# Differential attention: rotation among the projections, heads written out, maxima of the next head ahead of the present head's mixing

## What is computed

```python
ql, kl, vl = project(hl)          # latent tokens, 8 heads, q and k of 2 x 64, v of 128
qc, kc, vc = project(hc)          # context tokens
ql, kl = apply_rope(ql, cos, sin), apply_rope(kl, cos, sin)      # only the latent ones
lam = exp(sum(lp[0]*lp[1])) - exp(sum(lp[2]*lp[3])) + lam_init
keys, vals = concatenate([kc, kl]), concatenate([vc, vl])        # 512 tokens
s = einsum('bqhmd,bkhmd->bhmqk', q, keys) * 64 ** -0.5           # m = 0, 1
p = softmax(s)
a = p[:, :, 0] - lam * p[:, :, 1]
o = einsum('bhqk,bkhe->bqhe', a, vals)
y = rmsnorm(o, subln) * (1 - lam_init)                           # then @ w_out
```

## Time and profile before

| | us |
|---|---|
| median of three runs | 2550.07 |
| the profiled execution, its time | 2550.66 |
| its span, from the first to the last instruction | 2549.0 |
| TensorE busy in the span | 2421.8 |
| VectorE busy | 828.5 |
| ScalarE busy | 528.4 |
| GpSimd busy | 195.4 |

### The profile page before, as it was taken

One profiled execution on the slowest core, in us unless ns is written; L12 is line 12 of the kernel. 1 busy time (PEld: TensorE's weight loads), 2 busy tenths in 40 slices (PEclk: granted clock), 3 DMA queues, 4 the chain that ended last, 5 costly groups with the idle time before them and its releaser, 6 DMA issues.

```text
span 2549.0 us, 31145 instructions
## 1 busy us (share of the span) xinstructions
PE 2421.8 (95%) x12399; PEld 1977.2 (78%) x12399; DVE 828.5 (33%) x1600; ACT 528.4 (21%) x1305; POOL 195.4 (8%) x268
## 2 busy tenths in 40 slices
PE   5999999999998999899999999999999999678998
PEld 3788888864556988778888888888888867367887
DVE  4233310164545777253333013433301200731001
ACT  2111110122233444331111103111110211431001
POOL 1100000001022232000001000000000000100000
PEclk7999999999999999999999999999999999988999
DMA  8554462412210000134446523522452231023462
GB/s 271 199 174 156 163 169 73 136 53 81 67 50 17 1 1 1 50 117 148 165 151 192 168 68 106 186 95 82 128 136 68 89 116 66 0 66 119 158 173 62
DMA packets 277449, 275.56 MB, mean 108 GB/s; under 512 B 6505, under 2 KB 258019, under 8 KB 277219
## 3 DMA queue, kind: packets, MB, share of 16 engines
q1 hardware_dynamic: 256611, 198.60, 25.6%
q0 software_dynamic: 20736, 75.51, 8.4%
HBM read 273.04 MB, written 1.05 MB: 108 GB/s over the span
## 4 chain that ended last, share of the span: by engine, by line
PE 91%; DVE 4%; ACT 3%; issue 2%; DMA 1%; SPq 0%; POOL 0%; POOLq 0%; DVEq 0%; ACTq 0%
PE bank L714 32%; PE bank L859 18%; PE bank L609 12%; PE bank L879 6%; PE bank L905 3%; PE bank L1026 2%; PE bank L681 2%; PE bank L587 2%; PE bank L1185 2%; PE bank L1033 2%; PE bank L964 1%; PE bank L1040 1%; PE bank L989 1%; ACT hs L1571 1%; DVE room L2003 1%
## 5 line engine op out<-in xcount | busy, mean ns | idle before, releaser
L859 PE MATMUL bank<-big,ring 128*128 128x256 f32 x2112 | 458.8, 379 | 0.0
L859 PEld LDWEIGHTS bank<-big,ring 128*128 128x128 f32 x2112 | 400.4, 190 | 53.9
L714 PE MATMUL bank<-hs,ring 128*128 128x256 f32 x1584 | 378.3, 384 | 1.3 <-ACT hs L1316 1.3
L714 PEld LDWEIGHTS bank<-hs,ring 128*128 128x128 f32 x1584 | 300.1, 192 | 52.2 <-issue 11.3
L714 PE MATMUL bank<-room,big 128*128 128x256 f32 x1056 | 252.5, 382 | 0.0
L609 PE MATMUL bank<-hs,ring 128*128 128x512 f32 (+2 forms) x592 | 231.6, 548 | 0.0
L714 PEld LDWEIGHTS bank<-room,big 128*128 128x128 f32 x1056 | 201.8, 192 | 28.1 <-DVE room L1780 0.5
L2188 DVE TENSOR_TENSOR room<-room 128x256 f32<-128x256 f32 x70 | 29.8, 425 | 521.0 <-ACT room L1607 521.0
L609 PEld LDWEIGHTS bank<-hs,ring 128*128 128x128 f32 (+1 forms) x592 | 109.8, 188 | 107.6 <-issue 104.1
L472 POOL DMA_DIRECT2D mring<-in_w_mod x144 | 76.2, 529 | 1084.1 <-PE bank L587 1009.8
L879 PE MATMUL bank<-hs,ring 128*128 128x256 f32 x704 | 153.9, 382 | 1.6 <-ACT hs L1316 1.6
(11 more groups left out here) (277 smaller groups left out, 2826.2 us busy)
## 6 DMA issues: line engine op xcount, KB each, us to landing
ring<-in_ffn_w_in SPq DMA_DIRECT2D x88, 1024.0 KB, 5.0
mring<-in_w_mod POOLq DMA_DIRECT2D x144, 512.0 KB, 5.4
ring<-in_ffn_w_out SPq DMA_DIRECT2D x44, 1408.0 KB, 7.0
ring<-in_gdn_w_in SPq DMA_DIRECT2D x16, 1024.0 KB, 5.5
ring<-in_diff_w_in SPq DMA_DIRECT2D x12, 1024.0 KB, 5.1
ring<-in_gdn_w_out SPq DMA_DIRECT2D x4, 1024.0 KB, 4.9
ring<-in_diff_w_out SPq DMA_DIRECT2D x4, 1024.0 KB, 4.9
cst<-in_consts SPq DMA_DIRECT2D x1, 1344.0 KB, 9.5
```

The source lines that it names most:

```text
L714: last = mm(bank[:, (g0 + b) % 4, 0:LAT], w[:, k, jj * P:(jj + 1) * P], rhs[:, k, :], start=start and k == 0, stop=(k == KC // 2 - 1), ski ...
L859: last = mm(bank[:, g % 4, 0:LAT], w[:, k, :], big[:, k, cols], start=(k == 0), stop=(k == FC - 1))
```

## The change

The rotation leaves the heads. `turn_back(i)` and `rotary(i)` now handle one key or query block each (i = 0 to 7 keys, 8 to 15 queries) and write the result back to `big` in place. TensorE issues the first two behind `first_four`, one behind each of the twelve following groups of keys and queries, and the last two behind the first two groups of values. VectorE runs its 16 rotations ahead of everything for lambda. `scores` reads q and k from `big` directly, and the values product reads `v_rows`, so GpSimd's copies are gone. The heads are written out one by one on all engines. VectorE runs `maxima(h+1)` and then `mix(h)`; ScalarE runs `exps(h+1)` ahead of the copies of head h. Scores of head 0 no longer wait for lambda. `oat`, `rat` and the bank of the values product alternate between two buffers. New waits guard the transposes (`a_copied` of the head before), the mix (`a_turned` of the head before) and the copies (`attn_done` of the head before).

```diff
@@ room
-        qrot = carve(LAT)
-        rtmp = carve(2, LAT)
-        rtmp2 = carve(2, LAT)
-        vhead = [carve(NC, P), carve(NC, P)]
-        kall = [carve(TOK), carve(TOK)]
+        rtmp = [carve(LAT), carve(LAT)]
+        rtmp2 = [carve(LAT), carve(LAT)]
...
-        oat = carve(LAT)
-        rat = carve(LAT)
+        oat = [carve(LAT), carve(LAT)]
+        rat = [carve(LAT), carve(LAT)]
@@ GpSimd
             pool.wait_ge(S["head_closed"], HEADS + 2)
-            for par in range(2):
-                k_fix(par, par)
-                v_fix_rows(par, par)
...
+            for h in range(HEADS):
+                of("attn_root", h, 1, 1)
+                nc.gpsimd.tensor_tensor(big[:, h + 3 * KC, 0:LAT], oat[h % 2], rat[h % 2], ALU.mult).then_inc(S["head_closed"], 1)
@@ TensorE
+                    def turn_back(i):
+
+                        pe.wait_ge(S["acc_freed"], g0 + i + 1 + 4)
+                        if i > 1:
+                            pe.wait_ge(S["rotated"], i - 1)
+                        x = big[:, KC + i, CTX:TOK] if i < KC else big[:, i - KC, 0:LAT]
+                        mm(bank[:, 4 + i % 2, 0:LAT], k_("rot"), x, start=True, stop=True).then_inc(S["turned_back"], 1)
+
+                    for i in range(2):
+                        turn_back(i)
...
+                                turn_back(part * 8 + 2 * r + jj - 2)
...
+                            if r == 0 and t < 2:
+                                turn_back(2 * KC - 2 + t)
...
-                    def scores(n, par, first=False):
-                        of("k_fixed", n, 1, 1)
-                        of("rotated", n, 2, 2)
+                    def scores(n):
...
-                    def one_head(h, par, more):
-                        if more:
-                            turn_back(h + 1)
-                            scores(h + 1, 1 - par)
+                    def attend(h):
                         for t in range(2):
                             of("mixed_done", h, 2, t + 1)
+                            if h:
+                                of("a_copied", h - 1, 2, t + 1)
...
+                    pe.wait_ge(S["rotated"], 2 * KC)
+                    scores(0)
                     pe.wait_ge(S["head_closed"], HEADS + 2)
-                    turn_back(0)
-                    scores(0, 0, first=True)
-                    heads_of(lambda n: pe.Fori(0, n), one_head)
+                    pe.wait_ge(S["acc_freed"], g0 + 32 + 4)
+                    for h in range(HEADS):
+                        if h + 1 < HEADS:
+                            scores(h + 1)
+                        attend(h)
@@ ScalarE
+                    exps(0, range(4))
+                    act.wait_ge(S["head_closed"], HEADS + 2)
+                    for h in range(HEADS):
+                        if h + 1 < HEADS:
+                            exps(h + 1, range(4))
+                        copy_a(h)
+                        leave(h)
+                        root(h)
@@ VectorE
+                    def rotary(i):
+
+                        x = big[:, KC + i, CTX:TOK] if i < KC else big[:, i - KC, 0:LAT]
+                        dve.wait_ge(S["acc_freed"], g0 + i + 1 + 4)
+                        steps.did(v_.tensor_tensor(rtmp[i % 2], x, k_("cos"), ALU.mult))
+                        dve.wait_ge(S["turned_back"], i + 1)
+                        steps.link(v_.tensor_tensor(rtmp2[i % 2], bank[:, 4 + i % 2, 0:LAT], k_("sin"), ALU.mult))
+                        v_.tensor_tensor(x, rtmp[i % 2], rtmp2[i % 2], ALU.add).then_inc(S["rotated"], 1)
+
+                    for i in range(2 * KC):
+                        rotary(i)
+
...
+                            if h:
+                                of("a_turned", h - 1, 2, t + 1)
...
-                        if more:
-                            maxima(h + 1, 1 - par)
...
+                    maxima(0)
+                    for h in range(HEADS):
+                        if h + 1 < HEADS:
+                            maxima(h + 1)
+                        mix(h)
```

More of the change, by code:

```diff
@@ L1206, in scores @@
                                 rows = slice(m * HALF, (m + 1) * HALF)
-                                if not first:
+                                if n:
                                     of("probs_done", n - 1, 4, 2 * t + m + 1)
-                                mm(bank[:, 4 + 2 * t + m, :], qrot[rows, t * P:(t + 1) * P], kall[par][rows, :], start=True, stop=True).then_inc(S["scores_done"], 1)
-                    def one_head(h, par, more):
-                        if more:
-                            turn_back(h + 1)
-                            scores(h + 1, 1 - par)
+                                mm(bank[:, 4 + 2 * t + m, :], big[rows, n, t * P:(t + 1) * P], big[rows, n + KC, :],
+                                   start=True, stop=True).then_inc(S["scores_done"], 1)
+                    def attend(h):
                         for t in range(2):
                             of("mixed_done", h, 2, t + 1)
+                            if h:
+                                of("a_copied", h - 1, 2, t + 1)
                             for kt in range(NC):
@@ L1574, in one_head, with copy_a @@
-                    def one_head(h, par, more):
+                            fn(probs[n % 2][:, k, :], bank[:, 4 + k, :], ACT.Exp, bias=st[:, 4 + k:5 + k], scale=HALF ** -0.5,
+                               accum_out=st[:, 8 + k:9 + k]).then_inc(S["probs_done"], 1)
+                    def copy_a(h):
                         for t in range(2):
                             of("a_turned", h, 2, t + 1)
+                            if h:
+                                of("attn_done", h - 1, 1, 1)
@@ L1577, in one_head, with leave @@
                             fn(at_[:, :, t * P:(t + 1) * P], bank[:, 2 + t, :].rearrange("p (k q) -> p k q", k=NC),
                                ACT.Copy).then_inc(S["a_copied"], 1)
-                        if more:
-                            exps(h + 1, 1 - par)
+                    def leave(h):
                         of("attn_done", h, 1, 1)
-                        act.wait_ge(S["head_closed"], h + (HEADS + 2))
-                        fn(oat, bank[:, 1, 0:LAT], ACT.Copy, scale=lamv[:, 6:7])
@@ L1585, in one_head @@
-                        fn(rat, bank[:, 1, 0:LAT], ACT.Square).then_inc(S["attn_squared"], 1)
-                        of("attn_sum", h, 1, 1)
[L1587 to L1595, removed]
+                        if h > 1:
+                            act.wait_ge(S["head_closed"], h + (HEADS + 1))
@@ new lines, in leave, with root @@
+                        fn(oat[h % 2], bank[:, h % 2, 0:LAT], ACT.Copy, scale=lamv[:, 6:7])
+                        fn(rat[h % 2], bank[:, h % 2, 0:LAT], ACT.Square).then_inc(S["attn_squared"], 1)
+                    def root(h):
+                        of("attn_sum", h, 1, 1)
+                        inv_root(rat[h % 2], bank[:, h % 2, LAT:2 * LAT], eps_col[:, 0:1], 1.0 / P).then_inc(S["attn_root"], 1)
+                    exps(0, range(4))
+                    act.wait_ge(S["head_closed"], HEADS + 2)
@@ L2163, in one_head @@
                                                     ALU.mult, ALU.add).then_inc(S["mixed_done"], 1)
-                        if more:
-                            maxima(h + 1, 1 - par)
-                    rotary(0, 0)
-                    maxima(0, 0)
-                    @contextmanager
-                    def pairs(n):
-                        with steps.loop(n, 2 * (2 * 3 + 3 + 4)) as it:
-                            yield it
-                    heads_of(pairs, one_head)
+                    maxima(0)
[3 more added lines that the diff above has]
+                        mix(h)
                     go = g0 + 32
```

69 lines of the change are left out of this document (17 added, 52 removed).

## The result

The changed kernel took 2574.39 us (median of five runs, 2569.80 to 2579.54) beside 2552.84 for the kernel before on the same chips: a ratio of 1.009, 95% interval 1.0069 to 1.0111. It is 21.6 us slower; the forecast was 18.0 slower, 2568, and the range 2556 to 2582 holds the time. Since the kernel before stood at 2550.07 when the forecast was made, the time is 6.4 us above 2568 and the difference 3.6 above 18.0. The profiled execution took 2574.39 us, 23.7 more than that of before.

What follows compares the result with a forecast made beforehand. The prediction took TensorE, busy 95% of the span, as the bound. Heads of 112.8 us (11.1 more) and 6.9 in the projections gave +18.0 on 2550.1, near 2568 us; range 2556 to 2582.

Steps and rivals of the forecast that it cites:

- The projections: In the attention projections, where TensorE never waits, the 16 moved rotation matmuls cost their full 6.9 us.
- The start: From the projections' end to the ones of head 0: 17.5 us middle, 16.3 high, 18.6 low, against 21.96 before.
- The single line: In each head's period, ones, scores, maxima, mix and the steps after it follow in line: 12.24 us at high clock.
- tail: From the end of a head's mix through turns, copy, values and two ScalarE instructions to the ones: 4.23 us.
- the middle: Period of a head with about half at each clock level: 14.2 us, between 12.24 and 16.2; chance 58%.
- the last head: From the ones of head 6 to those of head 7: 7.1 us middle, 5.8 high, 8.5 low, against 7.83.
- the end: After the ones of head 7, until the output projection starts: stays 3.0 us, 2.6 at the high clock.
- low throughout: Period of a head with the clock at the low level all through: 16.2 us.
- the second rival: In the heads, one short clock fall per head at the old price of 1.05 us: +11.7, 2562 us; chance 20%.
- the third: Rival: in the heads the clock is low throughout, +32.5 us, 2583 us; chance 10%.
- the clock stays high: Rival: start and last head give back most of what the period and 16 matmuls cost: +3.3, 2553 us; chance 8%.
- the matmuls hide: Rival: the moved matmuls are hidden in the projections and the clock stays high: -3.6, near 2546.5 us; chance 4%.

Runs made afterwards that it cites:

- the second set of 16: The changed kernel with each of the 16 rotation matmuls issued twice: 2582.37 us, ratio 1.0131 to the kernel before.
- the run with work in the wait: The changed kernel with eight matmuls whose result nobody reads put between scores of h+1 and turns of h: 2560.64 us, ratio 1.0046.
- the run that moves nothing else in the heads of before: The kernel before, heads written out, with VectorE's maxima(h+1) moved between rotary(h+1) and the mix of h: 2587.61 us, ratio 1.0151.
- both orders mended: The changed kernel with VectorE's mix(h) ahead of maxima(h+1) and ScalarE's copies of h ahead of exponentials of h+1: 2524.44 us, ratio 0.9911.

## Why the prediction was right

**The projections.** Forecast 6.9 us, measured 6.84 in the trace, and 6.90 for the second set of 16. VectorE was busy 19.0 us there, forecast 21: a rotation takes 1.2 us.

**The start.** Forecast 17.5 us up to the ones of head 0 (16.3 high, 18.6 low), measured 2182.84 - 2164.76 = 18.08. Maxima began 2.36 us after the projections, forecast 2.29. VectorE ran both sets of maxima and the mix of head 0 in one go, as forecast. The turns and the values of head 0 were at the low clock. The scores of head 1 took 3.39 us instead of 1.99 at a clock of 1.00 (2168.95 to 2172.34): they follow the exponentials of head 0, which free their banks one by one (first wait 2.20 us). VectorE's maxima lagged behind them, so this cost nothing.

**The period.** The single line was there link by link: first maximum 1.16 us behind the scores (1.04 forecast), from the first maximum to the mix 3.15 (3.34), mix 3.09, tail at the high clock 4.23. The terms are off by 0.1 to 0.2 us in both directions (ones to scores 0.63, 0.54 forecast) and nearly cancel: the period, 12.24 in the forecast, was measured as 12.26 in the run with work in the wait. That the order does it, and neither the moved matmuls nor the written-out code, is shown by the run that moves nothing else in the heads of before (+40 us), by the swap on VectorE alone in the changed kernel (16 to 20 us less), by both orders mended with the moved matmuls left where they are (46 to 50 less), and by the written-out heads alone (no difference).

**The clock.** This is the term that was mis-sized. "I take 14.2, the middle" assumed about half of the time at each level in every part of the period. Measured: (2272.71 - 2182.84) / 6 = 14.98. The reason is where the low stretches lie. They are not spread evenly: turns and values, which follow the wait, were low in every one of the eight heads (about 2.3 us each; those of head 7 still from the fall ahead of head 6's turns), and in two of the six periods the ones and the scores were low as well (16.1 us each). 6 x 0.78 = 4.7 us of the 5.9 by which the heads exceeded the 112.8 forecast come from here, 1.1 from the last head for the same reason (8.23 against 7.1), 0.6 from the start; the end was 0.5 shorter. The bound "low throughout", 16.2, was met by two single periods (16.10, 16.12), although the clock stood at 1.00 for some 3 us of them: in that stretch TensorE only waited.

**The range.** 2556 to 2582 also holds the time of the second rival (2562) and ends just below that of the third (2583). So the hit by itself says little; what carries the explanation are the links of the period and the runs.

**The rivals.** That the clock stays high (2553 us) is excluded by 0.70 in the heads. One short fall per head at the old price of 1.05 us had nearly the right count (seven falls in eight heads) and the wrong price: the fall comes just ahead of the turns and the values, and costs 0.5 us on the turns and 1.8 on the values. The Trainium skill, TensorE: Matmul & The Clock Gate, section "Why this matters for your kernels", has it that an idle gap between bursts brings the clock down and dense work brings it back. The trace agrees in direction: after waits of 2.7 to 4.0 us for the mix the turns are low in all seven cases, and filling those waits with matmuls raised the clock of the heads from 0.70 to 0.94. That the matmuls hide is excluded by the doubled set; besides, the 3.6 us that this rival would have gained lie within the 7.65 us which the prediction itself calls no change, so its 4% did not belong to "faster". The clock low throughout (2583 us) is 9 us above the measured time.

**A gap in the argument.** I put the removal of the rotation at 1.6 us of a period, and saw only its price in the projections as a cost of its own. With the orders left alone the period is 7.7 us instead of 10.9. The forecast for this change did not need that, but it would have said which half of the change to keep.

## What to carry to other kernels

Where engines take their work in the order of the text and serve one chain, look first at whether work for the next item stands ahead of work for the present one; on VectorE and on ScalarE that order cost time here. The sign in the trace is two engines that wait for each other in turn, here VectorE for scores and TensorE for the mix. Cost a wait on TensorE with the clock of what follows it: here turns and values took 2.3 us more per head after some 4 us of waiting in front. And price the parts of a change apart: here one was worth 24 us and the other cost 46 to 50, and only their sum was visible in the result.

## What was not expected of the hardware

Work without a use made the kernel faster: 64 matmuls of 128x256, most of them in the waits, 11 to 14 us less in the time and a clock of 0.94 instead of 0.70 in the heads. And in the changed kernel shorter and longer periods alternate at first (14.51, 16.10, 14.51, 16.12 us) before two of 14.12 and 14.51, so one period is no measure of a head there; the mean of six is.
